# One weight tile unit ahead of a recurrence, its roundings on ScalarE, and smaller reference steps on VectorE

## What is computed

```
mod = silu(c) @ w_ada + b_ada                     # shifts, scales, gates
u = rmsnorm(x, norm1_w) * (1 + sc1) + sh1
hq, hf, hi, hg, aq, ak, av = split(u @ w_in)
f = lb + (1 - lb) * sigmoid(hf);  k = 1 - f
b = cumsum(log f) in a chunk                      # b_t, per head and channel
A[t,s] = sum_k q[t] k[s] exp(b_t - b_s), s <= t   # decay inside a chunk
o = A @ v + (q * exp(b)) @ S
S = exp(b_last) * S + (k * exp(b_last - b))^T @ v
...                                               # norm, differential attention, w_out, feed-forward, block two
```

## Time and profile before

| | |
|---|---|
| time, median of 3 runs | 1540.92 us (1538.4 to 1542.06) |
| the profiled execution's own time | 1538.91 us |
| its span | 1537.2 us |
| TensorE busy | 1463.1 us (95%) |
| VectorE busy | 986.6 us (64%) |
| ScalarE busy | 423.2 us (28%) |
| mean granted clock of TensorE | 0.983 |
| data moved | 175.80 MB, mean 114 GB/s |

### The profile page before, as it was taken

One profiled execution on the slowest core, in us unless ns is written; L12 is line 12 of the kernel. 1 busy time (PEld: TensorE's weight loads), 2 busy tenths in 40 slices (PEclk: granted clock), 3 DMA queues, 4 the chain that ended last, 5 costly groups with the idle time before them and its releaser, 6 DMA issues.

```text
span 1537.2 us, 19550 instructions
## 1 busy us (share of the span) xinstructions
PE 1463.1 (95%) x7186; PEld 1170.1 (76%) x7186; DVE 986.6 (64%) x1727; ACT 423.2 (28%) x901; POOL 95.5 (6%) x75
## 2 busy tenths in 40 slices
PE   3989999889999999998999999999998999999997
PEld 2777876667888888887876666778886888888886
DVE  8789888886767666556556666775546444444343
ACT  5333354432110110003234445531113221221011
POOL 0100000020000000222600000000030000000110
PEclk9999999999999999998999999999998999999999
DMA  9243232344556565543221111113331323233322
GB/s 374 80 156 110 69 138 77 96 144 153 192 195 193 194 195 157 153 126 121 73 69 42 48 50 42 49 49 109 96 110 55 109 84 107 92 99 89 103 86 93
DMA packets 52611, 175.80 MB, mean 114 GB/s; under 512 B 5953, under 2 KB 6337, under 8 KB 52545
## 3 DMA queue, kind: packets, MB, share of 16 engines
q1 hardware_dynamic: 52544, 174.94, 35.1%
HBM read 172.82 MB, written 2.10 MB: 114 GB/s over the span
## 4 chain that ended last, share of the span: by engine, by line
PE 51%; ACT 1%; DVE 1%; issue 0%; ACTq 0%; DVEq 0%
PE bank L628 11%; PE bank L630 11%; PE bank L629 11%; PE bank L1070 8%; PE bank L1089 2%; PE bank L1124 2%; PE bank L1101 2%; PE bank L640 1%; PE bank L641 1%; PE bank L642 1%; PE bank L1001 0%; DVE wl L1611 0%; PE bank L1114 0%; PE bank L1045 0%; PE bank L737 0%
## 5 line engine op out<-in xcount | busy, mean ns | idle before, releaser
L628 PE MATMUL bank<-uh,wh 128*128 128x512 f32 x808 | 316.0, 391 | 6.0 <-DVE wl L1611 4.8
L630 PE MATMUL bank<-uh,wl 128*128 128x512 f32 x808 | 315.1, 390 | 0.0
L629 PE MATMUL bank<-ul,wh 128*128 128x512 f32 x808 | 315.0, 390 | 0.0
L1609 DVE CAST wh<-wraw 128x1024 fp32r<-128x1024 f32 (+1 forms) x235 | 156.2, 665 | 196.8 <-PE bank L630 180.0
L1611 DVE TENSOR_TENSOR wl<-wraw,wh 128x1024 fp32r<-128x1024 f32 (+1 forms) x235 | 275.1, 1171 | 8.1
L628 PEld LDWEIGHTS bank<-uh,wh 128*128 128x128 f32 x808 | 152.1, 188 | 39.0 <-issue 4.9
L630 PEld LDWEIGHTS bank<-uh,wl 128*128 128x128 f32 x808 | 151.9, 188 | 31.9
L629 PEld LDWEIGHTS bank<-ul,wh 128*128 128x128 f32 x808 | 152.1, 188 | 31.4
L628 PE MATMUL bank<-hh,wh 128*128 128x512 f32 x352 | 137.5, 391 | 0.0
L630 PE MATMUL bank<-hh,wl 128*128 128x512 f32 x352 | 137.1, 389 | 0.0
L629 PE MATMUL bank<-hl,wh 128*128 128x512 f32 x352 | 137.0, 389 | 0.0
(11 more groups left out here) (355 smaller groups left out, 2331.6 us busy)
## 6 DMA issues: line engine op xcount, KB each, us to landing
ada<-in_w_ada_dram SPq DMA_DIRECT2D x96, 512.0 KB, 4.6
wraw<-in_w_in_dram SPq DMA_DIRECT2D x61, 512.0 KB, 3.4
wraw<-in_w_ffn_gate_dram SPq DMA_DIRECT2D x44, 512.0 KB, 3.3
wraw<-in_w_ffn_up_dram SPq DMA_DIRECT2D x44, 512.0 KB, 3.3
wraw<-in_w_ffn_down_dram SPq DMA_DIRECT2D x32, 512.0 KB, 3.5
wraw<-in_w_ffn_down_dram SPq DMA_DIRECT2D x16, 384.0 KB, 3.1
wraw<-in_w_out_dram SPq DMA_DIRECT2D x16, 256.0 KB, 2.8
wraw<-in_w_out_dram SPq DMA_DIRECT2D x8, 512.0 KB, 3.4
```

What stands on the lines that cost most here:

```text
L628: nc.tensor.matmul(bank[:], a, rh[:, k0 + k, :], start=(first and k == 0), stop=False)
L629: nc.tensor.matmul(bank[:], a, rl[:, k0 + k, :], start=False, stop=False)
L630: mm = nc.tensor.matmul(bank[:], b, rh[:, k0 + k, :], start=False, stop=(last and k == nk - 1))
L1609: V.tensor_copy(wh[:, slot, 0:n], wraw[:, slot, 0:n]).then_inc(w_hi, 1)
```

## The change

1. One whole a1 unit (number 8) is worked ahead of the recurrence; the other thirteen are spread over the 32 slots, 3, 3, 3 and 4 tiles in turn instead of 3 and 4. VectorE splits units 8 and 9 before the first scan. The load of unit 10 is asked for ahead of four rows of `w_ada`.
2. ScalarE rounds units 10 to 22 (`cast_next`); VectorE only makes the rest.
3. Level 0 and the decay to the chunk's end are not written out as exponents: ScalarE reads `bb` and takes the reference as its bias, 8 instructions of 64 columns and 4 of 128 a head in place of 2 of 256 and 1 of 512. VectorE writes only four negated references (128x4) in place of a 128x512 difference, and the other 128x512 difference (L1932) is gone.
4. ScalarE keeps the output of head h after level 2 of head h+1, not before `vtm`.
5. The setup steps of VectorE go from k = 1 to k = 3, those of ScalarE from k = 2 to k = 5.

```diff
-        SLOT_END = [A1_UNITS * KT * (p + 1) // SLOTS for p in range(SLOTS)]
+        SLOT_END = [KT + (A1_UNITS - 1) * KT * (p + 1) // SLOTS for p in range(SLOTS)]
...
-        DRAIN_AT = {slot_of(KT * n + KT - 1) + 2: n for n in range(A1_UNITS)}
-        SPLIT_AT = {slot_of(KT * n - 1) + 1 if n else 0: n for n in range(A1_UNITS)}
+        DRAIN_AT = {slot_of(KT * n + KT - 1) + 2 if n else 0: n for n in range(A1_UNITS)}
+        SPLIT_AT = {slot_of(KT * n - 1) + 1 if n > 1 else 0: n for n in range(1, A1_UNITS)}
...
             load_unit(ph, 0, 0)
             load_unit(ph, 0, 1)
+            load_unit(ph, 1, 0)
             for j in range(16, 16 + MSLOTS):
                 load_mod(j)
-            for n in range(2, len(TILES["a1"])):
+            for n in range(3, len(TILES["a1"])):
...
+            a1_tiles(0, KT)
             for h in range(HEADS1):
...
-                    a1_slot(n)
+                    a1_tiles(SLOT_END[n - 1] if n else KT, SLOT_END[n])
...
-                if k == 2:
+                if k == 5:
                     act.wait_ge(setup_v, 5)
                     A(lsc[:, 4:12], lsc[:, 4:12], ACT.Exp)
...
+                if lv == 0:
+                    for c in range(NT):
+                        mid, end = c * P + P // 2, (c + 1) * P
+                        A(xx[:, 0, mid:end], bb[:, mid:end], ACT.Exp, bias=nref[:, c:c + 1])
+                        mm = A(xx[:, 0, c * P:mid], bb[:, c * P:mid], ACT.Exp, bias=bb[:, mid - 1:mid], scale=-1.0)
+                    mm.then_inc(g_e, 1)
...
+                elif lv == 7:
+                    act.wait_ge(g_qk, 14 * h + 12)
+                    A(xx[:, 1], bb[:], ACT.Exp).then_inc(g_e, 1)
                 else:
-                    src, dst = (bb[:], xx[:, 1]) if lv == 7 else (xx[:, 0], xx[:, 0])
-                    A(dst, src, ACT.Exp).then_inc(g_e, 1)
+                    act.wait_ge(g_qk, 14 * (h + 1))
+                    for c in range(NT):
+                        cc = slice(c * P, (c + 1) * P)
+                        mm = A(xx[:, 0, cc], bb[:, cc], ACT.Exp, bias=bb[:, (c + 1) * P - 1:(c + 1) * P], scale=-1.0)
+                    mm.then_inc(g_e, 1)
+
+            def cast_next(n):
+
+                u = PH["a1"].u0 + n + 1
+                act.wait_ge(w_hi, u)
+                act.wait_ge(w_in[u % 2], 16 * (u // 2 + 1 - FRONT // 2))
+                act.wait_ge(unit_done, u - 1 + U1)
+                A(wh[:, u % 2, :], wraw[:, u % 2, :], ACT.Copy).then_inc(w_hi, 1)
 
             def drains_of_slot(p):
+                if p in SPLIT_AT and p % 8 != 6:
+                    cast_next(SPLIT_AT[p])
                 if p in DRAIN_AT:
                     a1_drain(DRAIN_AT[p])
...
+                    if lv == 7 and 8 * h + 6 in SPLIT_AT:
+                        cast_next(SPLIT_AT[8 * h + 6])
                     exp_level(h, lv)
+                    if lv == 2 and h:
+                        keep_output(h - 1)
                     drains_of_slot(8 * h + lv - 1)
...
-                if k == 1:
+                if k == 3:
                     l0, l1 = vt1[:, LB:LB + 4], vt1[:, LB + 4:LB + 8]
...
-                split(u, u % 2)
+                v.wait_ge(w_hi, u + 1)
+                V.tensor_tensor(wl[:, u % 2, :], wraw[:, u % 2, :], wh[:, u % 2, :].bitcast(F32),
+                                ALU.subtract).then_inc(w_split, 1)
+                for j in MOD_AFTER.get(u, ()):
+                    modulation(j)
...
+            def references():
+
+                V.tensor_scalar(nref, bb[:, P // 2 - 1:T:P], -1.0, None, ALU.mult).then_inc(g_x, 1)
...
             forget(0)
-            split(8, 0)
+            split(PH["a1"].u0, 0)
+            split(PH["a1"].u0 + 1, 1)
             v.wait_ge(const_ok, 5 + 2)
             decay_sums(0)
-            exponents(0)
+            references()
...
-                v.wait_ge(g_qk, 14 * (h + 1))
-                V.tensor_tensor(xx[:, 0].rearrange("p (c t) -> p c t", c=NT),
-                                bb[:].rearrange("p (c t) -> p c t", c=NT)[:, :, P - 1:P].broadcast_to([P, NT, P]),
-                                bb[:].rearrange("p (c t) -> p c t", c=NT), ALU.subtract).then_inc(g_x, 2)
```

More of the change, by code:

```diff
@@ L222, in build @@
         eps2, rcolr = tiny[:, 38:39], tiny[:, 34:38]
+        nref = tiny[:, 34:38]
         std, rcol, stdr = tiny[:, 50:54], tiny[:, 54:58], tiny[:, 58:62]
@@ L778, in _, with a1_tiles @@
                     front_tile(n, k)
-            def a1_slot(p):
+            def a1_tiles(x0, x1):
                 ph = PH["a1"]
-                for n, k in (divmod(x, KT) for x in range(SLOT_END[p - 1] if p else 0, SLOT_END[p])):
+                for n, k in (divmod(x, KT) for x in range(x0, x1)):
                     if k == 0:
@@ L1314, in exp_level @@
             def exp_level(h, lv):
-                act.wait_ge(g_x, 9 * h + lv + 1)
                 if lv < 7:
+                    act.wait_ge(g_x, 7 * h + lv + 1)
+                if lv == 0:
[4 more added lines that the diff above has]
+                    mm.then_inc(g_e, 1)
+                elif lv < 7:
                     m = LEVELS[lv]
@@ L1336, in _, with keep_output @@
                     exp_level(0, 0)
+            def keep_output(h):
+                act.wait_ge(g_o, h + 1)
+                A(p1[:, 8 + h, :], B[2][:], ACT.Copy)
+                for c in range(NT):
+                    if h or c:
+                        act.wait_ge(ss_ok, 4 * h + c)
+                    mm = A(junk[:, 0:P], B[2][:, c * P:(c + 1) * P], ACT.Square,
+                           scale=SQ_SCALE, accum_out=ssh[:, 4 * h + c:4 * h + c + 1])
+                    mm.then_inc(ss_ok, 1)
             for h in range(HEADS1):
@@ L1356, in _ @@
                     a1_drain(A1_UNITS - 1)
[L1357 to L1364, removed]
+            keep_output(HEADS1 - 1)
             def da_exps(m):
```

## The result

The changed kernel takes 1547.53 us (median of 7 runs, 1544.92 to 1550.22) against 1540.92; the ratio is 1.0044 with a 95% interval of 1.0035 to 1.0054. The median lies 0.03 us above the range that was given, and the forecast, 1542.0, said "no difference".

The account below looks back on a forecast made before the run. TensorE was taken to set the recurrence's pace, VectorE close behind. -6.0 lead + 12.7 new waits - 5.5 old waits = +1.2 us on 1538.9, 1540.1; plus 2.0 for the median, 1542.0 us; 8-in-10 range 1535 to 1547.5.

Parts of the forecast that it names:

- The front (-3.5): Stage before the recurrence: 2.47 us from earlier rests plus 1.70 from the kept clock, less 0.65 at unit 7.
- pause of 1.8 us: Front, before unit 4: TensorE would stand still 1.8 us, where it was 4.3, and keep 2.4 GHz.
- the 1.7 us: Front, first matmuls of unit 4: 1.70 us saved if TensorE keeps 2.4 GHz behind its pause; lost at 1.2 GHz.
- Unit 8 ahead, L804 at 76.5, slot 1 at 83.07: Recurrence's start: unit 8 fills TensorE's pause; by slot 1 the changed kernel is 6.0 us ahead, the front included.
- The waits at the splits: Recurrence: TensorE waits for products behind ScalarE's roundings; 2.8 us at slot 9, 2.0 at 11, 1.8 at 26.
- The sum: Whole change: 6.0 us of lead and 5.5 of old waits gone against 12.7 of new waits, +1.2 us.
- the 5.5 of before: Recurrence of the kernel before: TensorE's waits for VectorE, 5.5 us start to start, all taken to go.
- the references: Heads' beginnings: ScalarE's small exponentials with a bias, hidden except for 0.3 to 0.9 us a head, 1.5 in all.
- that TensorE keeps 2.4 GHz through the pauses in slots 1 and 9: Recurrence: the forecast charged no lower clock behind pauses of 3.1 and 2.8 us, leaving that to a rival.
- the lower clock: Rival: pauses at slots 1 and 9 each draw 1.2 GHz, costing 1.6 to 1.7 us; 1545.4 us, chance 0.17.
- That a freed VectorE does not help: Recurrence splits: VectorE's saved 8.6 us count only where it is late; new waits are for ScalarE and unit_done.
- The rival that would have made it faster: Recurrence: VectorE, freed of 8.6 + 4.2 us, keeps split waits from TensorE; -7 us, 1534 to 1535, chance 0.16.

Follow-up runs that it names:

- e2: The kernel before with only the setup steps of VectorE and ScalarE moved to k = 3 and k = 5; 1537.16 us.
- e6: The changed kernel with idle matmuls added on TensorE in its waits at slots 1 (12), 9 (10) and 11 (8); 1543.46 us.
- e3: The changed kernel with idle matmuls added on TensorE in its waits at slots 9 (10) and 11 (8); 1546.14 us.
- e4: The changed kernel with the setup steps put back at k = 1 and k = 2; 1552.45 us.
- e5: The changed kernel with a head's output again kept ahead of the next head's `vtm`; 1550.05 us.
- e10: The changed kernel with VectorE again writing the differences of level 0 and the chunk's end, and 2 and 1 exponentials; 1548.81 us.
- e1: The changed kernel with VectorE again rounding units 10 to 22 itself; 1535.93 us.
- e9: The changed kernel, ScalarE still rounding, with each row of `mod` moved one slot later, behind products and merge; 1535.71 us.
- e8: The changed kernel with VectorE rounding again and each row of `mod` moved one slot later; 1529.21 us.
- e7: The kernel before with only the rounding of units 9 to 22 moved to ScalarE, old slot table; 1548.51 us.

## Why the prediction was wrong, point by point

- **The front (-3.5)** was right: e2 measures 3.5 us by the medians (3.3 in its trace, counted from the first matmul), and its pause of 1.85 us kept the higher clock, as forecast. In the changed kernel the last matmul of the front starts at 70.98 instead of 74.24 us, and unit 7 waited 0.54 us for the last `xn` (0.65 forecast). But in its trace there was no pause of 1.8 us to keep the clock through (last section), so that there the 1.7 us came out by another way than was worked out.
- **Unit 8 ahead, L804 at 76.5, slot 1 at 83.07** was right to 0.2 us in the trace; the lead there was 5.8 us (6.0 forecast). The terms as written add up to 83.0, not 83.07.
- **The waits at the splits** were right in place and nearly in size. Recorded at slots 1, 9, 11 and 26: 3.0, 2.4, 2.1, 1.35 (forecast 3.1, 2.8, 2.0, 1.8, from start to start, which is 0.1 to 0.2 longer than a record); the records of slots 4, 6 and 19 and of the end of head 1 (0.76, 1.51, 0.76, 1.48) are within 0.2 of the forecast too. The sum was low by 1.3 to 1.5 us: e6, at full clock, is 2.5 us above the kernel before by the medians and 2.7 in its trace, where the sum said 1.2. Start to start the ten new waits add up to 14.5 us instead of 12.7. About 0.9 of the difference is at the later heads' beginnings (slots 8, 16 and 24): the waits that stood there before, 0.6 us each, did not go with "the 5.5 of before", and the references added about 0.5 to them, not 1.5. The rest is 0.2 to 0.3 more at slots 4, 6, 11, 14, 19 and 21.
- **The step that failed** is the one that was left to a rival: that TensorE keeps 2.4 GHz through the pauses in slots 1 and 9. The prediction gave the lower clock 0.17 and 1545.4 us, though one of its own rows (a pause of 2.9 us with 0.69 in the window) stood against the forecast, and it did not price the clock behind the pause of 2.1 us at slot 11 at all. In the changed kernel's trace slots 9 and 11 drew the lower clock and slot 1 did not; in e3, e4, e5 and e10 slot 1 did. e6 measures what the clock costs: 4.1 us by the medians, 3.4 in the traces, 1.6 to 1.7 a stretch, which is the price that the rival had. With that, the sum of 1542.0 would have been 1545.4 to 1546.1, and the likeliest case "slower"; the rest to 1547.53 is mostly the 1.3 to 1.5 us of the waits. The Trainium skill ("TensorE: Matmul & The Clock Gate", HAM oscillation) was right in kind: it tells of matmul bursts with waits between them, each burst starting cold, though the waits in its case, 3 to 5 us, are longer than these. The traces agree only in part: not every burst behind such a pause started at the lower clock, but one to three a recurrence did in the kernels that had pauses of 2 to 3 us there (e6 apart, where they were filled).
- **That a freed VectorE does not help** was right: e1 against the changed kernel shows that the roundings moved to ScalarE cost 11.6 us, the lower clock included, rather than gave anything. In e1 VectorE waits 4.5 us for units to end before it may round, so it has nothing to gain there; and ScalarE's rounding is longer (1.05 against 0.69 us) and stands behind `vtm` and exponentials. The prediction named each of these waits but never set edit 2 alone against leaving it out, and so did not see that one edit turned a gain into a loss.
- **The rival that would have made it faster** (0.16) fell; the one of the front that gives nothing (0.12) too.
- **Nothing changes behind the recurrence** held for the changed kernel (1327.7 us both). In nine of the twelve other traces the same code took 1.9 to 2.8 us more.

## What to carry to other kernels

Where one engine feeds another through a chain that starts with an event, count the chain's length, not the engines' sums: moving a step to an idle engine helps only if the chain gets shorter, and a step in it that nobody waits for yet (here a row of 1.2 us) should stand behind what is waited for. Do not price TensorE's pauses of 2 us and more by their length alone. A stretch at the lower clock behind one cost 1.6 us here (slots 9 to 13 of e3 took 3.2 us less than the changed kernel's, with two stretches gone), and nine of the twelve pauses of 2.0 to 3.1 us in the recurrences of the changed kernel, e3, e4, e5 and e10 drew one. Of the pauses up to 1.74 us in any recurrence none did.

## What the runs showed of the hardware that was not expected

- The same pause draws the lower clock in one execution and not in the next. Slot 1's 3.0 us did not in the changed kernel and did in e3, which is the same program up to slot 9, and in e4, e5 and e10; slot 9's 2.4 us did in the changed kernel and e4 and not in e10; slot 11's 2.1 us did in the changed kernel, e4 and e10 and not in e5; 1.81 us at slot 1 did in e9, and 1.7 us at slot 11 of e1 did not. So the length alone does not decide; what does, these runs do not show.
- The stage behind the recurrence, unchanged, took 1327.2 to 1330.5 us over these traces, and in the main its clock goes with it. Added up over windows of 4 us, what the granted clock lacked to 1 was 12.0 us in the changed kernel and 13.6 before (1327.7 us both), 17.1 in e8 (1330.4) and 17.0 in e1 (1330.3). So a difference of up to 3 us between two single executions can come from unchanged code.
- The lower level lasted mostly about 3.5 us, and about 7 in e7 (78 to 84.7), e5 (121 to 128) and e10 (83 to 90).
- In the changed kernel's front matmuls started every 0.43 us up to 30.34 us (in the kernel before only up to 25.5), though the granted clock of the window from 20 to 40 us is recorded as 1.00. So near the start of a trace the spacing of the matmuls shows the level, and the recorded figure does not. It cost nothing here: the last of unit 3 starts at 31.88, and the first of unit 4, which needs a rest that VectorE began at 30.88, at 32.16. That is where the pause went that was forecast at 1.8 us: TensorE spent it working slowly, and began unit 4 at the higher clock. e2 had the pause itself, 1.85 us, and the higher clock behind it too.

```profile
29.91 0.63 PE L765 MATMUL bank<-ul,wh 128*128 128x512 f32 x1
30.34 0.56 PE L766 MATMUL bank<-uh,wl 128*128 128x512 f32 x1
30.73 0.40 PE L764 MATMUL bank<-uh,fh 128*128 128x512 f32 x1
...
31.88 0.39 PE L766 MATMUL bank<-uh,fl 128*128 128x512 f32 x1
32.16 0.50 PE L764 MATMUL bank<-uh,fh 128*128 128x512 f32 x1
```
